# Passage from the up to the down products: GpSimd makes a hidden operand's low part ahead of a weight sum's, and TensorE opens the second down product before the first one's last k

## The reference

```python
def sqrelu_mlp(h, w_up, w_down):          # w_up 1024 x 4096, w_down 4096 x 1024
    return jnp.square(jax.nn.relu(h @ w_up)) @ w_down

for i in range(DEPTH):                    # DEPTH = 2
    ...                                   # x += mixer(rms_norm(x))
    x = x + sqrelu_mlp(rms_norm(x), w_up[i], w_down[i])
```

## Time and profile before

| | before |
|---|---|
| median of 3 runs | 1460.09 us (1458.02 to 1461.18) |
| profiled execution | 1457.89 us |
| its span, first to last instruction | 1456.0 us |
| mean granted TensorE clock | 0.994 |
| TensorE matmuls busy | 1417.1 us, 10168 instructions |
| VectorE, ScalarE, GpSimd busy | 992.2, 722.9, 849.0 us |

### The profile page before, as it was taken

The page is one execution under the profiler, slowest core; times in us unless marked ns, Lnnn a source line. Parts: engine busy times, 40 slices in busy tenths (PEclk is TensorE's granted clock), DMA queues, the critical chain, the costliest instruction groups (busy, mean ns, idle before and its releaser), DMA issues.

```text
span 1456.0 us, 29349 instructions
## 1 busy us (share of the span) xinstructions
PE 1417.1 (97%) x10168; PEld 1332.2 (91%) x10168; DVE 992.2 (68%) x1787; ACT 722.9 (50%) x1506; POOL 849.0 (58%) x634
## 2 busy tenths in 40 slices
PE   9999999998999999999999999999989999999999
PEld 7889999998999999999988778787989999999999
DVE  6006716776867768778777676868668678687784
ACT  4423200125735537456537585766257356474562
POOL 8554455443866758667787052442437668576683
PEclk9999999999999999999999999999999999999999
DMA  7322232220222322222443110101202222322222
GB/s 237 107 85 73 72 112 72 72 72 30 88 88 88 106 97 86 86 87 86 142 129 92 30 45 16 43 14 43 73 30 88 88 88 88 112 88 89 87 87 94
DMA packets 36541, 120.46 MB, mean 83 GB/s; under 512 B 6056, under 2 KB 6760, under 8 KB 36208
## 3 DMA queue, kind: packets, MB, share of 16 engines
q1 hardware_dynamic: 32320, 111.83, 22.9%
q10 hardware_dynamic: 4144, 7.65, 1.7%
HBM read 115.91 MB, written 3.55 MB: 82 GB/s over the span
## 4 chain that ended last, share of the span: by engine, by line
PE 55%; POOL 19%; issue 17%; DVE 5%; ACT 3%; POOLq 0%; DVEq 0%; ACTq 0%
POOL w_lo L751 17%; PE ps L865 9%; PE ps L867 8%; PE ps L866 8%; PE ps L1032 6%; PE ps L1034 6%; PE ps L1033 6%; PE ps L1392 2%; POOL op_lo L757 2%; PE ps L1209 2%; PE ps L1332 1%; PE ps L1007 1%; PE ps L1335 1%; PE ps L974 1%; PE ps L1214 1%
## 5 line engine op out<-in xcount | busy, mean ns | idle before, releaser
L751 POOL TENSOR_TENSOR w_lo<-raw,w_hi 128x512 fp32r<-128x512 f32 x256 | 350.2, 1380 | 200.6 <-ACT w_hi L2199 199.9
L1032 PE MATMUL ps<-op_hi,w_hi 128*128 128x288 f32 x896 | 267.3, 298 | 18.9 <-POOL op_lo L757 18.9
L1033 PE MATMUL ps<-op_lo,w_hi 128*128 128x288 f32 x896 | 265.8, 297 | 0.0
L1034 PE MATMUL ps<-op_hi,w_lo 128*128 128x288 f32 x896 | 264.9, 296 | 0.0
L715 POOL TENSOR_SCALAR w_hi<-raw 128x1024 fp32r<-128x1024 f32 x75 | 83.3, 1111 | 270.8 <-PE ps L867 120.0
L2199 ACT CAST w_hi<-raw 128x512 fp32r<-128x512 f32 x256 | 159.1, 623 | 123.9 <-PE ps L1034 123.2
L717 POOL TENSOR_TENSOR w_lo<-raw,w_hi 128x1024 fp32r<-128x1024 f32 x75 | 186.6, 2488 | 6.2
L1032 PEld LDWEIGHTS ps<-op_hi,w_hi 128*128 128x128 f32 x896 | 169.2, 189 | 20.8 <-POOL op_lo L757 20.8
L1034 PEld LDWEIGHTS ps<-op_hi,w_lo 128*128 128x128 f32 x896 | 170.1, 190 | 0.0
L1033 PEld LDWEIGHTS ps<-op_lo,w_hi 128*128 128x128 f32 x896 | 169.5, 189 | 0.0
L1032 PE MATMUL ps<-x_hi_four,w_hi 128*128 128x288 f32 x512 | 152.1, 297 | 2.0 <-DVE ps L1711 2.0
(11 more groups left out here) (252 smaller groups left out, 3844.1 us busy)
## 6 DMA issues: line engine op xcount, KB each, us to landing
raw<-stream SPq DMA_DIRECT2D x207, 512.0 KB, 3.6
x<-xt SPq DMA_DIRECT2D x8, 288.0 KB, 7.5
out_x<-x ACTq DMA_DIRECT2D x8, 288.0 KB, 2.2
b_bc<-bs ACTq DMA_DIRECT2D x2, 512.0 KB, 7.0
cache_raw<-cache_ct ACTq DMA_DIRECT2D x1, 1024.0 KB, 5.8
v_out<-sgu_grow ACTq DMA_DIRECT2D x1, 512.0 KB, 5.0
ws_sb<-ws ACTq DMA_DIRECT2D x2, 256.0 KB, 5.3
out_v<-v_out ACTq DMA_DIRECT2D x1, 512.0 KB, 4.7
```

Source lines behind the costliest of these rows:

```text
L751: nc.gpsimd.tensor_tensor(block_of(w_lo, f), factor(n, f), block_of(w_hi, f).bitcast(F32), ALU.subtract).then_inc(w_low_set, 1)
L1032: nc.tensor.matmul(out, l_hi, r_hi, start=first, stop=False, skip_group_check=True)
L1033: nc.tensor.matmul(out, l_hi, r_lo, start=False, stop=False, skip_group_check=True)
L1034: done = nc.tensor.matmul(out, l_lo, r_hi, start=False, stop=last, skip_group_check=True)
```

## The change

On GpSimd, in every up step, the low part of slots 3 and 4 of this step's hidden operands goes ahead of the low part of the weight sum S4. On TensorE, in the passage, the first three k of A12 run before the last k of A11. On VectorE and ScalarE the sums, low parts, casts and additions of the passage change places: the addition of product A11 goes ahead of slot 1's low part and of the third sum, and the low part of slot 6 ahead of the fourth sum; ScalarE's cast of slot 1 waits for the second sum instead of the third.

```diff
@@ GpSimd, quarter, up step n
                     low_block(mlp, q, n + 1, A12)
                     low_block(mlp, q, n + 1, S3)
+                    low_hidden(mlp, q, n, 3 * n + 1, slice(3, 5), slice(0, 2))
                     low_block(mlp, q, n + 1, S4)
-                    low_hidden(mlp, q, n, 3 * n + 1, slice(3, 5), slice(0, 2))
                     low_block(mlp, q, n + 1, A22)
@@ TensorE
                 def first_down(q):
-                    n = PAIRS
+                    n, last = PAIRS, (PAIRS - 1,)
                     weights(q, n, A11)
                     operand(q, PAIRS - 1)
                     operand_pool(q, 2 * PAIRS - 3)
-                    product(n, A11, before_last=lambda: operand_pool(q, 2 * PAIRS - 1))
+                    product(n, A11, range(PAIRS - 1))
                     weights(q, n, A12)
-                    product(n, A12, before_last=lambda: operand(q, PAIRS))
+                    product(n, A12, range(PAIRS - 1))
+                    operand_pool(q, 2 * PAIRS - 1)
+                    product(n, A11, last)
+                    operand(q, PAIRS)
+                    product(n, A12, last)
                     weights(q, n, S1)
@@ VectorE, down, i == 0
                         operand_sum(q, e, 1)
-                        operand_sum(q, e, 2)
-                        low_operands(q, e, 3 * e + 3, slice(1, 2), A)
                     add(A11, i, first, X)
                     if i == 0:
-                        operand_sum(q, e, 3)
-                        h = 4 * (e % 2)
-                        low_operands(q, e, 3 * e + 4, slice(6, 7), hb[:, h + 3:h + 4, :])
+                        low_operands(q, e, 3 * e + 3, slice(1, 2), A)
+                        operand_sum(q, e, 2)
                     elif more:
                         last_sums(mlp, q, n + 1, 0)
                     add(A12, i, first, Y)
                     if i == 0:
+                        h = 4 * (e % 2)
+                        low_operands(q, e, 3 * e + 4, slice(6, 7), hb[:, h + 3:h + 4, :])
+                        operand_sum(q, e, 3)
                         low_operands(q, e, 3 * e + 5, slice(2, 3), E)
@@ ScalarE, down, i == 0
                     if i == 0:
-                        cast_banks(q, e, 3, slice(1, 2), A)
+                        cast_banks(q, e, 2, slice(1, 2), A)
                         cast_sums(q, e, 3)
```

## The result

| | before | changed |
|---|---|---|
| median | 1459.05 us (4 runs, 1457.81 to 1461.18) | 1438.17 us (4 runs, 1436.79 to 1439.86) |
| profiled execution | 1457.89 us | 1439.86 us |
| its span | 1456.0 us | 1438.0 us |

The ratio is 0.9856 with a 95% interval of 0.9837 to 0.9875: 20.9 us less by the medians, where 19.8 was forecast. A second set of four runs of the same changed kernel gave 1438.49 us, where the kernel before gave 1457.85 us in the same set: 19.4 us less.

The account below looks back on a forecast made before the run. TensorE, with work for 97% of the span, was taken as the bound. Gains of 2.10 us at eight passages (16.8) plus 3.0 for slow clock stretches, 19.8 us together, gave a median of 1440.3 us, range 1435.5 to 1448.

Parts of the forecast that it names:

- GpSimd's and TensorE's halves: At each up to down passage: 1.23 us from GpSimd's earlier low part, 1.20 from A12 matmuls put into TensorE's gap.
- Up to S1: TensorE in the passage, from A11 to S1: S1 starts at 493.82 instead of 496.25, a gain of 2.43 us.
- Given back: Waits before the last k of S1 and S2 on VectorE's low parts: 0.33 us a passage, bounds 0 and 2.2.
- Slow stretches: Granted clock 0.50 after TensorE's restart, in the first quarter of each MLP: 1.50 us each, both gone, 3.0 us.
- Rival 1: In the passage GpSimd takes the SBUF port before VectorE, S2's last k starts 0.5 us later: 1444.4 us, chance 0.18.
- Rival 3: The wait moves: waits among TensorE, ScalarE and VectorE come to 1.3 us a passage: 1448.3 us, chance 0.12.
- the ring: TensorE, ScalarE and VectorE waiting on one another in the passage, with under 0.1 us of spare.
- Rival 2: The slow clock stretches after TensorE's restarts stay, 3.0 us more: 1443.3 us, chance 0.10.
- rival 4: A11's last k waits as long as before, for something that GpSimd hid: near 1460 us, chance 0.04.
- Rival 5: In all 32 up steps GpSimd's moved low part waits for a later ScalarE cast: slower, 1464.3 us, chance 0.04.
- Cover: A22's low and SP's weight loads keep their time; VectorE, some 2 us behind TensorE after the passage, costs nothing.
- The opening step: In each MLP's first up step GpSimd waits for a cast, about 0.5 us later, twice; idle time covers it.

## Why the prediction was right

- **What bounds it.** Right. TensorE's waits were the whole matter: their 18.9 us went from the list, and matmuls' busy time stayed.
- **GpSimd's and TensorE's halves.** 1.23 and 1.20 us forecast. Alone they brought 1.23 and 1.02 to 1.05, where the second was expected to carry a restart at S1.
- **Up to S1.** From A11's start to S1's start 3.48 us were measured (398.97 to 402.45) and 3.40 forecast (490.42 to 493.82), so the gain up to there is 2.35 us and not 2.43. GpSimd's low part took 1.44 us for the 1.40 of the row, and A12's last k had a small restart of its own, 0.17 us to its second matmul.
- **Given back.** 0.33 us forecast: 0.18 at S1 and 0.15 at S2. Measured from A11's last k at 401.50: S1's last k 2.17 later, forecast 2.18, and 0.15 us lost there (0.04 and 0.11). At S2 there is no pause, since slot 6's low part ended 3.68 us after A11's last k instead of 3.88: VectorE had the port first, 0.46 us for the 0.64 that I took from the row. The mis-sized term: S2's 0.15 is 0. By these rows 2.35 - 0.15 = 2.20 us; a quarter became 2.23 us shorter, forecast 2.10.
- **Slow stretches.** 3.0 us forecast from the two spacings of restarts. They went, and the first to second passage fell by 3.75 us, which is 2.23 and 1.5. That the pause is the cause was argued then. It is shown now: present at 2.4 us, absent at 1.1 us and 0.14 us, back with 2.4 us under the new order and with a pause of 2.45 us of another cause. A long pause alone isn't enough, though, since six of eight had no slow stretch behind them; what else it takes stays open.
- **The sum.** 8 x 2.23 + 3.0 = 20.8 us against 20.9 measured by the medians; forecast 19.8. That 20.8 and 20.9 agree so well is luck: the second set gave 19.4 us, and the two profiled executions differ by 18.0. In the latter the changed kernel's first passage begins 2.3 us later (A11 at 398.97 against 396.71), and between the two MLPs it gains 1.6 us where 2.2 was due. The time came to 1438.2 against 1440.3: 1.1 us by the larger gain, and 1.0 because the forecast started from the median of three runs, 1460.1, and a fourth brought it to 1459.05.
- **Rivals.** Rival 1: the port is taken in turn, but VectorE won, 0.04 us ahead at all eight passages. Where GpSimd was first, in the kernel with VectorE as before, ScalarE's cast came earlier and covered it; so its price of 4.1 us was never seen. Rival 3: the ring exists, with one restart of 0.12 us a passage instead of 1.3. Rival 2 fell with the slow stretches, and rival 4 with the wait. Rival 5 fell for this change, but its mechanism is real: one place further ahead, a late cast delays SP's loads. It then costs 3.8 us, at a single passage and by way of VectorE's weight sum, not at each of 32 steps.
- **Cover.** A22's low and SP's loads kept their place: VectorE waits 2.7 us in all for weight loads, 0.6 at most. VectorE behind TensorE cost nothing.
- **The opening step.** The 0.5 us forecast for it is there, and costs nothing. In the second profiled run of the changed kernel, whose opening has the pace of the kernel before's, GpSimd's low part waits for its cast and starts at 362.87, where S4's started at 362.36:

```profile
362.87 1.43 POOL L757 TENSOR_TENSOR op_lo<-hb,op_hi 128x576 fp32r<-128x576 f32 x1 [1.86 <-ACT op_hi L2296]
```

  SP's loads follow at 366.83 instead of 366.33. GpSimd's idle time ahead of its next low part of slots 5 and 6 shrinks from 3.45 to 2.88 us, which takes up the delay, and the first passage is no later (A11 at 396.65 against 396.71).

## What to carry to other kernels

When one engine idles for a part that another makes late, look at both lists: what stands ahead of the part, and what work could stand ahead of the wait. Here the two gains added, up to nearly the pause's length. Then replay what was hidden behind the long wait, with the durations and hand-over times of the rows: here the replay was right within 0.2 us, and it tells when to stop, since past that point a move gains a tenth of a microsecond a passage or uncovers the next late part. In an order written by hand, the price of moving an instruction ahead is paid by what stands behind it, down to the transfers that another queue issues on its count.

## What the hardware showed that was not expected

The runs of one kernel spread over 1.6 to 5.4 us, and where two traces were compared most of that was not from the passages. Granted clock in the opening of the first MLP, in two runs of one and the same changed kernel, the first with a span of 1438.0 and the second with 1435.5 us:

```profile
348.00:352.00 4.00, 4.00 (x23) 4.00 (x23) 0.58 (x1) 2.32 (x3) 1.43 (x1) 0.65 0.32 85
352.00:356.00 4.00, 2.53 (x12) 2.43 (x12) 2.78 (x7) 1.46 (x4) 1.28 (x1) 0.50 0.45 181
356.00:360.00 4.00, 4.00 (x19) 3.62 (x18) 2.35 (x7) 1.24 (x3) 0.38 (x1) 0.57 0.00 0
```

```profile
348.00:352.00 4.00, 3.45 (x28) 3.35 (x27) 1.06 (x5) 2.36 (x4) 1.43 (x1) 1.00 0.33 88
352.00:356.00 4.00, 3.08 (x14) 2.90 (x15) 4.00 (x9) 1.57 (x4) 1.28 (x1) 0.68 0.44 178
356.00:360.00 4.00, 3.00 (x18) 2.61 (x18) 2.04 (x5) 2.62 (x6) 1.56 (x2) 0.90 0.00 0
```

The longer slow stretch of the first run puts its first passage 2.3 us later (slot 5's low part at 404.76 against 402.44), before the changed part of TensorE's list is reached. That is 2.3 of the 2.5 us between the two spans. What sets off the longer stretch stays open. For effects of a microsecond the distance between two like places of one trace, which repeats within 0.05 us in the changed kernel and within 0.1 in the others where no slow stretch lies near, is a better measure than the median.
